# The mLSTM's running maximum spread by two 256-column products into the scores' banks, and the key transposes moved behind the scores

## What is computed

```python
b = jnp.cumsum(lf, axis=-1)
logD = where(tri, b[..., :, None] - b[..., None, :] + ig[..., None, :], -inf)
m_t = maximum(b + m[..., None], logD.max(axis=-1))
D = exp(logD - m_t[..., None])
inter = exp(b + m[..., None] - m_t)
S = einsum('bhtd,bhsd->bhts', q, k) * D
num = inter[..., None] * einsum('bhtd,bhde->bhte', q, C) + einsum('bhts,bhse->bhte', S, v)
den = inter * einsum('bhtd,bhd->bht', q, n) + S.sum(axis=-1)
h = num / maximum(abs(den), exp(-m_t))[..., None]
w = exp(b[..., -1:] - b + ig - m_new[..., None])
C_new = decay[..., None, None] * C + einsum('bhs,bhsd,bhse->bhde', w, k, v)
```

## Time and profile before

| | us |
|---|---|
| median of 3 runs | 2520.21 (2512.19 to 2523.08) |
| profiled execution, its own time | 2510.49 |
| its span | 2508.7 |
| PE busy | 2425.4 (97%) |
| PEld busy | 2034.8 |
| DVE busy | 1318.4 |
| ACT busy | 877.6 |
| mean granted TensorE clock | 0.99 |

### The profile page before, as it was taken

How to read it: one execution, slowest core, us unless ns; L and a number is a source line. 1 busy time by engine, 2 the same in 40 slices (tenths; PEclk the granted TensorE clock), 3 DMA queues, 4 the chain that set the end, 5 groups by cost and what they waited for, 6 DMA issues and landing times.

```text
span 2508.7 us, 32496 instructions
## 1 busy us (share of the span) xinstructions
PE 2425.4 (97%) x13093; PEld 2034.8 (81%) x13093; DVE 1318.4 (53%) x2611; ACT 877.6 (35%) x1568; POOL 66.3 (3%) x115
## 2 busy tenths in 40 slices
PE   6999999999999999999999999999999989999997
PEld 5887888888796888888998888888789769888885
DVE  4468544446367644446255844445636674444444
ACT  3344332233345423223334533233324533222221
POOL 2000000000000000000000300000000000000000
PEclk9999999999999999999999999999999999999999
DMA  5311223233411232323421232323523112222221
GB/s 184 90 47 58 93 93 101 93 109 119 136 54 51 85 96 92 98 93 119 143 71 34 66 101 93 98 93 110 162 50 118 34 55 89 81 76 76 81 79 63
DMA packets 176851, 224.77 MB, mean 90 GB/s; under 512 B 16652, under 2 KB 127509, under 8 KB 176685
## 3 DMA queue, kind: packets, MB, share of 16 engines
q1 hardware_dynamic: 164700, 190.34, 24.5%
q10 hardware_dynamic: 6560, 22.55, 2.6%
q0 software_dynamic: 5440, 9.80, 1.4%
HBM read 211.30 MB, written 12.60 MB: 89 GB/s over the span
## 4 chain that ended last, share of the span: by engine, by line
PE 82%; DVE 9%; ACT 3%; DMA 2%; issue 2%; ACTq 0%; SPq 0%; DVEq 0%
PE ps L1839 25%; PE ps L1841 24%; PE ps L1840 24%; DMA w_raw<-in_w_in_dram 2%; PE ps L1918 2%; DVE w_lo L1057 1%; PE ps L1898 1%; DVE a_lo L1061 1%; PE ps L1907 1%; DVE x L1061 1%; ACT w_hi L645 1%; DVE wide L1108 1%; ACT PT L687 1%; DVE w_lo L1053 1%; PE ps L1937 1%
## 5 line engine op out<-in xcount | busy, mean ns | idle before, releaser
L1839 PE MATMUL ps<-a_hi,w_hi 128*128 128x512 f32 (+2 forms) x1688 | 591.6, 351 | 12.8 <-DVE w_lo L1057 7.7
L1841 PE MATMUL ps<-a_hi,w_lo 128*128 128x512 f32 (+2 forms) x1688 | 592.8, 351 | 0.0
L1840 PE MATMUL ps<-a_lo,w_hi 128*128 128x512 f32 (+2 forms) x1688 | 591.3, 350 | 0.0
L645 ACT ACTIVATE w_hi<-w_raw 128x1024 fp32r<-128x1024 f32 (+1 forms) x336 | 333.1, 1032 | 600.9 <-PE ps L1841 550.7
L1057 DVE TENSOR_TENSOR w_lo<-w_raw,w_hi 128x1024 fp32r<-128x1024 f32 (+1 forms) x336 | 400.2, 1197 | 178.5 <-ACT w_hi L645 177.8
L1839 PE MATMUL ps<-w_hi,u_hi 128*128 128x512 f32 (+1 forms) x1088 | 431.0, 396 | 10.4 <-DVE x L1061 10.4
L1841 PE MATMUL ps<-w_hi,u_lo 128*128 128x512 f32 (+1 forms) x1088 | 430.8, 396 | 0.0
L1840 PE MATMUL ps<-w_lo,u_hi 128*128 128x512 f32 (+1 forms) x1088 | 430.1, 395 | 0.0
L1839 PEld LDWEIGHTS ps<-a_hi,w_hi 128*128 128x128 f32 x1688 | 321.3, 190 | 57.2 <-issue 12.0
L1061 DVE TENSOR_TENSOR x<-x,ps 128x512 f32<-128x512 f32 x272 | 185.4, 685 | 322.1 <-PE ps L1841 322.1
L1840 PEld LDWEIGHTS ps<-a_lo,w_hi 128*128 128x128 f32 x1688 | 319.2, 189 | 41.9
(11 more groups left out here) (316 smaller groups left out, 1979.9 us busy)
## 6 DMA issues: line engine op xcount, KB each, us to landing
w_raw<-in_w_up_dram SPq DMA_DIRECT2D x128, 512.0 KB, 3.8
w_raw<-in_w_down_dram SPq DMA_DIRECT2D x128, 512.0 KB, 3.5
w_raw<-in_w_out_dram SPq DMA_DIRECT2D x32, 512.0 KB, 4.2
w_raw<-in_w_in_dram SPq DMA_DIRECT2D x24, 580.0 KB, 4.2
w_raw<-in_w_in_dram SPq DMA_DIRECT2D x24, 512.0 KB, 3.8
w_raw<-in_w_in_dram SPq DMA_DIRECT2D x32, 256.0 KB, 3.1
x<-in_x_prompt_dram ACTq DMA_DIRECT2D x12, 512.0 KB, 6.3
wide<-in_x_prompt_dram ACTq DMA_DIRECT2D x12, 512.0 KB, 4.1
```

Of the source, the lines that this page charges most:

```text
L645: eng.activation(w_hi[b][:, k * n:(k + 1) * n], raw[p % RAW][:, 0:n], ACT.Copy).then_inc(w_high.sem, 1)
L1839: eng.matmul(out, lh, rh, start=(k == ks[0]), stop=False)
L1840: eng.matmul(out, lh, rl, start=False, stop=False)
L1841: ins = eng.matmul(out, ll, rh, start=False, stop=(k == last))
```

## The change

- The one 512-column product of a single row becomes two products of 256 columns, one with its row on partition 0 (heads 0 and 2), one on partition 64 (heads 1 and 3). They write columns 256 to 511 of banks 5 and 7, beside the scores, and stand behind the scores instead of ahead of them.
- ACT's exponentials of `inter` read there. DVE's mask add becomes two adds of 256 columns.
- Bank 4 is free, so the keys are turned into it, and `turn_keys(j + 1)` stands right behind `relate(j + 1)`, ahead of the second `op_step`. It waits for kw(j) (`kw_ok`), because kw(j) reads the same bank. `turn_keys(0)` stands behind `relate(0)`, ahead of the first `op_step`.
- The wait for the state (`c_ok`) moves from `turn_keys` to `state_sums`.
- `Mline` has two partitions in use; its four DMAs go by head. A constant square that nothing reads is left out, and the constants come in two DMAs.

```diff
 def lines(q):
-    for j in range(BLK):
-        pool.dma_start(Mline[32 * j:32 * j + 1, :].rearrange("p (h t) -> p h t", h=HM), Mrel[:, j, :]).then_inc(m_line.sem, 16)
+    for h in range(HM):
+        i, par = h // 2, h % 2
+        pool.dma_start(Mline[par * DK:par * DK + 1, :, i, :], Mrel[h:h + 1, :, :]).then_inc(m_line.sem, 16)
 # SP, start
-sp.dma_start(square[:, :, :], c_square).then_inc(first_in.sem, 16)
+for dst, src in ((square[:, 0:2, :], c_square[:, 0:2, :]), (square[:, 2:4, :], c_square[:, 3:5, :])):
+    sp.dma_start(dst, src).then_inc(first_in.sem, 16)
 # ACT, block j
-src = ps[4][rs, :].rearrange("p (i g t) -> p g i t", g=2, i=2)[:, par]
+src = max_at(par)[rs, :].rearrange("p (i t) -> p i t", i=2)      # ps[5 + 2 * par][:, 256:512]
 # DVE, relate(q, j)
-tt(DT[:, :, :], ps[4][:, :]..., cmask..., ALU.add).then_inc(m_add.sem, 1)
+for par in range(2):
+    own = DT[:, :, :].rearrange("p (i r) t -> p r i t", r=2)[:, par]
+    ins = tt(own, max_at(par).rearrange("p (i t) -> p i t", i=2), cmask..., ALU.add)
+ins.then_inc(m_add.sem, 1)
 # DVE, kw(j)
-tt(kw[:, :, :], ps[6][:, 0:HM * DK]..., cols[:, 2, j, :]..., ALU.mult).then_inc(kw_ok.sem, 1)
+tt(kw[:, :, :], ps[4][:, 0:HM * DK]..., cols[:, 2, j, :]..., ALU.mult).then_inc(kw_ok.sem, 1)
 # PE
 def relate(q, NT, j):
-    eng.matmul(ps[4][:, :], ones[row, :], Mline[row, :], start=True, stop=True).then_inc(m_out.sem, 1)
     for h in range(HM):
         ...
     ins.then_inc(s_out.sem, 1)
+    for par in range(2):
+        row = slice(par * DK, par * DK + 1)
+        ins = eng.matmul(max_at(par), ones[row, :], Mline[row, j, :, :].rearrange("p i t -> p (i t)"), start=True, stop=True)
+    ins.then_inc(m_out.sem, 1)
 def turn_keys(q, j):
     if j:
-        eng.wait_ge(c_ok.sem, c_ok.at(q, j))
-    else:
-        eng.wait_ge(on_ok.sem, on_ok.at(q, BLK))
+        eng.wait_ge(kw_ok.sem, kw_ok.at(q, j))
     for i in range(2):
-        ins = eng.transpose(ps[6][:, i * P:(i + 1) * P], zT[:, 6 + i, j * P:(j + 1) * P], ident[:, :])
+        ins = eng.transpose(ps[4][:, i * P:(i + 1) * P], zT[:, 6 + i, j * P:(j + 1) * P], ident[:, :])
 def state_sums(q, j):
     eng.wait_ge(kw_ok.sem, kw_ok.at(q, j + 1))
+    if j:
+        eng.wait_ge(c_ok.sem, c_ok.at(q, j))
+    else:
+        eng.wait_ge(on_ok.sem, on_ok.at(q, BLK))
 def turn_heads(q, j):
+    if heads_bank(j) == 4:
+        eng.wait_ge(kw_ok.sem, kw_ok.at(q, BLK))
 relate(q, NT, 0)
+turn_keys(q, 0)
 for j in range(BLK):
     for _ in range(plan[j][0]):
         op_step(o)
-    turn_keys(q, j)
     numerators(q, j)
     if j + 1 < BLK:
         relate(q, NT, j + 1)
+        turn_keys(q, j + 1)
     for _ in range(plan[j][1]):
         op_step(o)
     state_sums(q, j)
```

More of the change, by code:

```diff
@@ L175, in hymba_layer @@
         x1 = sb("x1", [P, BLK + 1, D])
-        square = sb("square", [P, 5, P])
-        ident, triu, ntriu, cmask, ones = (square[:, i, :] for i in range(5))
+        square = sb("square", [P, 4, P])
+        ident, triu, cmask, ones = (square[:, i, :] for i in range(4))
         bias = sb("bias", [P, H, 2 * P])
@@ L191, in hymba_layer @@
         st = sb("st", [P, 240])
-        rows = sb("rows", [96, BLK, P])
-        kwin = sb("kwin", [P, KVH * DH])
-        Mline = sb("Mline", [3 * 32 + 1, HM * P])
+        rows = sb("rows", [P, BLK, P])
+        kwin = rows[:, 0, :]
+        Mline = sb("Mline", [DK + 1, BLK, 2, P])
         gz = sb("gz", [P, BLK + 1, 2 * HM])
@@ L230, in hymba_layer @@
         eps_col = st[:, 146:147]
-        srow = Mline[0:HM, 0:5 * NS].rearrange("p (i t) -> p i t", i=5)
+        srow = Mline[0:HM, :, :, :].rearrange("p j i t -> p (j i t)")[:, 0:5 * NS].rearrange("p (i t) -> p i t", i=5)
         def flat(t):
@@ L316, in hymba_layer @@
         h_ok, h_sq, hn_ok, h_out = signal("h_ok", BLK), signal("h_sq", BLK), signal("hn_ok", BLK), signal("h_out", BLK)
-        m_line = signal("m_line", 16 * BLK)
+        m_line = signal("m_line", 16 * HM)
         carried = signal("carried", 2, 1)
@@ L498, in heads_bank, with max_at @@
             return (4, 5, 7, 2)[j]
+        def max_at(par):
+            return ps[5 + 2 * par][:, 2 * P:4 * P]
         def tmp_tile(n):
@@ L1488, in relate @@
                 eng.wait_ge(ib_ok.sem, ib_ok.at(q, j + 1))
-                tt(DT[:, :, :], ps[4][:, :].rearrange("p (h t) -> p h t", h=HM), cmask.unsqueeze(1).broadcast_to([P, HM, P]), ALU.add).then_inc(m_add.sem, 1)
+                for par in range(2):
+                    own = DT[:, :, :].rearrange("p (i r) t -> p r i t", r=2)[:, par]
+                    ins = tt(own, max_at(par).rearrange("p (i t) -> p i t", i=2), cmask.unsqueeze(1).broadcast_to([P, 2, P]), ALU.add)
+                ins.then_inc(m_add.sem, 1)
                 if j:
@@ L1685, in quarter @@
                         eng.wait_ge(c_out.sem, c_out.at(q, j))
[L1686 removed]
+                    tt(kw[:, :, :], ps[4][:, 0:HM * DK].rearrange("p (h d) -> p h d", h=HM), cols[:, 2, j, :].unsqueeze(2).broadcast_to([P, HM, DK]), ALU.mult).then_inc(kw_ok.sem, 1)
                     if j == BLK - 1:
@@ L1810, in _ @@
             eng.wait_ge(setup.sem, setup.at(0, 10))
-            eng.wait_ge(first_in.sem, first_in.at(0, 16 * 2))
+            eng.wait_ge(first_in.sem, first_in.at(0, 16 * 3))
             for b in range(2):
@@ L1934, in relate @@
                     eng.wait_ge(gained.sem, gained.at(q, BLK))
-                    eng.wait_ge(m_line.sem, m_line.at(q, 16 * BLK))
-                row = slice(32 * j, 32 * j + 1)
-                eng.matmul(ps[4][:, :], ones[row, :], Mline[row, :], start=True, stop=True).then_inc(m_out.sem, 1)
+                    eng.wait_ge(m_line.sem, m_line.at(q, 16 * HM))
                 for h in range(HM):
@@ L2000, in sample_pe @@
                     eng.wait_ge(s_rowsok.sem, s_rowsok.at(0, 1))
-                    eng.transpose(ps[6][0:NS, 0:96], rows[:, 0, 0:NS], ident[0:96, 0:96]).then_inc(s_cols.sem, 1)
+                    eng.transpose(ps[6][0:NS, 0:96], rows[0:96, 0, 0:NS], ident[0:96, 0:96]).then_inc(s_cols.sem, 1)
                     for h in range(HM):
@@ L2190, in quarter @@
                 for i in range(BLK):
-                    ins = eng.transpose(ps[0][:, i * 96:(i + 1) * 96], rows[:, i, :], ident[0:96, 0:96])
+                    ins = eng.transpose(ps[0][:, i * 96:(i + 1) * 96], rows[0:96, i, :], ident[0:96, 0:96])
                 ins.then_inc(g_cols.sem, 1)
```

## The result

| | before | after |
|---|---|---|
| median, 20 runs each | 2512.68 us (2505.64 to 2525.26) | 2521.18 us (2516.52 to 2529.75) |
| ratio to before, 95% interval | | 1.003 [1.0017, 1.0043] |
| profiled execution, its span | 2510.49, 2508.7 | 2524.9, 2523.1 |

The changed kernel is 0.3% slower. By the ratio that is 7.5 us, with an interval from 4.3 to 10.8; the two medians differ by 8.5. The sum of the steps had been +7.5, and the time forecast 2527, which is 5.8 above the measured median.

What follows compares the result with a forecast made beforehand. PE was taken as the bound, with 82% of the chain of waits. Stages +4.1 and start +0.4 gave +4.5, clock +3 made +7.5 us, added to the median 2520.21 for 2527; range 2514 to 2542.

Steps and rivals of the forecast that it cites:

- the pair in place of one product: On PE in each block: two 256-column products side by side take 0.65 us instead of 1.05, gaining 0.40 a block.
- the wait ahead of them: Ahead of block 1's key transposes: PE stands still for kw(0), 5.0 us, replacing waits of 1.50, 1.42 and 0.39.
- block 1: kw(1) comes well ahead, so no new wait; only the products' gain, -0.40 us.
- block 2, the wait; its sum: Quarters 0 to 2: PE waits about 0.88 us for kw(2); less the 0.40 gain, +0.48.
- block 2 in quarter 3: No split_vec ahead of kw(2), but DVE close behind: -0.20 us of the 0.40 gain.
- the four stages: The four quarters' mLSTM stages: +1.19 us in each of three, +0.51 in quarter 3, sum +4.1.
- start: Kernel start: SP issues one more DMA ahead of the gains, +0.4 us; bounds 0 and 0.5.
- clock: Half clock behind PE's 5.0 us idle in every quarter: 2.0 us lost each, 8.0, +3 against before; bounds 0 and 13.6.
- Rival 1: Single-row products do not pair; the maximum costs 1.05 us again, 3.4 on top: 2531; 12%.
- Rival 3: At the border of blocks 0 and 1: kw(0) is no new wait, waits merge into equal sum; -5 us, 2515; 10%.
- Rival 4: Nothing shows: stalls as forecast, clock falls no more often than before; +4.5 us, 2525; 65% together with the forecast.
- Rival 2: Slower by over 0.5%: every 5.0 us idle brings 6.82 us at half clock; +14.7 us, 2535; 13%.

Runs made afterwards that it cites:

- e8: Kernel before, with only the constants' load cut into two DMAs ahead of the gains; ratio 1.0011 [0.9994, 1.0028].
- e3: Changed kernel with both spreading products taking their row from partition 0; one run, 2522.55 us.
- e1: Changed kernel with the key transposes put back (bank 6, behind the first op_step, waiting for the state), the two products kept; 2511.62 us, 0.9989.
- e2: Changed kernel with turn_keys(j + 1) behind the second op_step, still in bank 4 and waiting for kw(j); 2511.02 us, 0.9989.
- e9: Changed kernel with its four constant squares in one DMA again; ratio 1.0037 [1.002, 1.0054].
- e4: Changed kernel with DVE making kw(j) right behind weigh(j), ahead of the op_step and the weights; 2518.8 us, 1.002.

## Why the prediction was right

The change of the time and its mechanism came as forecast. The time itself was forecast at 2527 and came to 2521.2, because the forecast was added to a median of 3 runs, 2520.21, and 20 runs of that kernel have 2512.68. That +7.5 met +7.5 is in part luck: the stage cost less than forecast, the start more, and the clock's share is only what is left over. The steps, at full clock in quarter 1 where no other is named:

| step | forecast | measured |
|---|---|---|
| the pair in place of one product | 0.65 | 0.63 |
| numerators(0) later | 0.3 | 0.32 (5.40 behind the first score) |
| block 1's transposes, behind the first score | 13.57 | 13.57 |
| the wait ahead of them | 5.0 | 4.89 |
| numerators(1), from the first score | 20.25 | 20.20 |
| block 1 | -0.40 | -0.55 (9.75; before, 10.30 in quarter 2 and 10.31 in e8) |
| block 2, the wait; its sum | 0.88; +0.48 | 0.86; +0.45 |
| block 2 in quarter 3 | -0.20 | -0.30 |
| the four stages | +4.1 | +3.1 |
| start | +0.4 | +1.4 at the first transposes |
| clock | +3 | +3.0 is left |

The +3.1 are the stages of the two profiles without what each lost at half clock (below): 182.01 less 6.7 against 176.95 less 4.7. By quarters it is 0.98, 0.97, 0.83 and 0.31.

**The product and the pair.** The value at the scores' end of the bounds was right, and e3 shows that the partition decides it. The Trainium skill ("TensorEngine Tiling (Array Packing)", Key Properties) says that tiles on other rows of the array compute in parallel. The runs agree, for a single row in each half: 0.63 on partitions 0 and 64, 1.05 on partition 0 alone. Rival 1 falls with it.

**The chain and the new wait.** These were read off the timelines of before, nearly all to a tenth. What made it possible was to ask of the moved transposes what is queued behind them, and to follow kw(0) back through DVE to ACT. Rival 3 falls: the waits that went summed to 3.3 us a quarter, the one that came is 4.9, and e1 and e2 show that the written order alone makes it.

**Start.** This term was mis-sized: +1.4 for 0.4. I priced the extra DMA by its issue. The gains were issued 0.48 later, but DVE could go on only 2.07 later, and 0.7 of that was swallowed ahead of PE. My upper bound of 0.5 was no bound. How much of it reaches the total is open: the first score of quarter 0 comes at 173.56 to 175.23 in the eight profiles with two DMAs and at 172.79 to 173.58 in the five with one, 1.1 apart on the mean, and e9's total shows no gain.

**Clock.** In the profile of after 6.7 us are lost: numerators(1) come later than at full clock by 1.65, 1.34, 1.85 and 1.87 in the four quarters. That is under the 8.0 forecast. The profile of before, read the same way, lost 4.7 (block 1 of quarters 0 and 1 took 1.60 and 3.12 more than the 10.31 of e8's quarter 0, which ran at full clock), where the prediction had 5.1. It also has a fourth window at half clock that the prediction passed over, at 175.26, and that one was free: it only shortened the wait for kw(0) to 0.31. So it is +2.0, which with the 3.1 makes the 5.06 of the windows. But the profiles alone do not settle this term. e9 has the waits of after and lost 9.0 (2.75, 2.70, 2.18, 1.39), and e8 has those of before and lost 9.5.

The mean granted clock of many runs is what speaks for it. It was 0.9861 in 20 runs of after, and between 0.9875 and 0.9886 in the sets of before beside the experiments (none is on record for the 20 runs of before beside after). Among the 29 runs of before in one set, 0.001 of mean clock went with 1.6 us, so this is 2 to 4 us; in e9 beside its own runs of before, 0.9853 against 0.9886, it is 5. The 3.0 left over from 7.5 less 3.1 less 1.4 lie in it. Whether it is 2 or 5 stays open. Rival 4, a clock that falls no more often than before, is unlikely by this, but the profiles do not exclude it. Rival 2 needed 3.3 lost in a quarter; it came to 1.9 at most in the profile of after and to 2.75 in e9's. In the profile of after the slow stretches begin inside the idle. Where one begins behind it, as in quarter 1 of e4 (772.90, 6.83 us, all busy), 3.2 are lost, near that rival's 3.4.

Not tried: the transposes moved early with the single product kept, for which no bank is free. Nor was a bank for the early transposes that kw does not read; e4, which takes the wait for kw away on DVE, shows that PE then stands ahead of numerators(1).

## What to carry to other kernels

Before you move an instruction that waits ahead of one that does not, name the work that used to run during the wait: here a step of 2.9 us was the cover of the chain to kw(0), and putting two transposes of 0.2 us ahead of it cost more than 0.4 a block saved on PE. A faster PE gains nothing in a stretch that ACT and DVE set; taking one weights unit out of their chain took 3.7 us off block 0 and brought 0.7% without any change on PE. And where idle of PE cannot be avoided, in short pieces with waits behind them it cost less clock here (e1) than in one piece with busy work behind it (e4).

## What the runs showed of the hardware

- Single-row f32 products on partitions 0 and 64 run side by side: 2 x 256 columns in 0.63 us, against 1.05 on one partition.
- The slow clock can begin inside an idle of 4.9 us (185.60, with the wait ending at 188.81) or behind one of 3.8 (772.90, with the wait ending at 771.70). How much of it hits running matmuls hangs on that: 3.62 of 6.83 us in the first case, all 6.83 in the second.
- The issue of two weights loads on SP took 1.43 us in the kernel before, and 4.65 and 4.77 with one small DMA more ahead of it (after, e8). Without that DMA the long issue falls on the load behind them (2.94 in the kernel before, 3.16 in e9). What waits for the gains came 2 us later.
- The four stages with the same code lost 6.7 and 9.0 us to the clock in two profiles (after, e9), and 4.7 and 9.5 in two others (before, e8).
